# A transformer block with product-key experts: load and router seams reordered, key distances squared by ScalarE in the U tiles with gate groups

## What is computed

```python
def peer(xn, wq, subkeys, u, v):
    def chunk_fn(xc):
        q = (xc @ wq).reshape(PEER_CHUNK, PEER_HEADS, 2, PEER_QDIM // 2)
        sc = jnp.einsum('thpd,pkd->thpk', q, subkeys)
        sv, si = lax.top_k(sc, PEER_TOPK)
        cand = sv[:, :, 0, :, None] + sv[:, :, 1, None, :]
        cv, ci = lax.top_k(cand.reshape(PEER_CHUNK, PEER_HEADS, PEER_TOPK * PEER_TOPK), PEER_TOPK)
        i1 = jnp.take_along_axis(si[:, :, 0], ci // PEER_TOPK, axis=-1)
        i2 = jnp.take_along_axis(si[:, :, 1], ci % PEER_TOPK, axis=-1)
        e = i1 * PEER_NKEYS + i2
        g = jax.nn.softmax(cv.astype(jnp.float32), axis=-1)
        act = jax.nn.gelu(jnp.einsum('td,thkd->thk', xc, u[e]))
        return jnp.einsum('thk,thkd->td', g * act, v[e])
```

## Time and profile before

| what | before |
|---|---|
| median of 3 runs | 1064.41 us |
| the profiled execution | 1065.53 us |
| its span | 1063.7 us |
| busy: TensorE, VectorE, ScalarE, GpSimd | 99%, 82%, 65%, 30% |
| one 128x512 square of ScalarE in the U groups (L1084), and one relu (L1101) | 0.62 us each |
| bytes moved | 181.36 MB, mean 170 GB/s |
| TensorE clock granted | full in all 40 slices |

### The profile page before, as it was taken

One profiled execution on the slowest core, in us unless ns is written; L12 is line 12 of the kernel. 1 busy time (PEld: TensorE's weight loads), 2 busy tenths in 40 slices (PEclk: granted clock), 3 DMA queues, 4 the chain that ended last, 5 costly groups with the idle time before them and its releaser, 6 DMA issues.

```text
span 1063.7 us, 22280 instructions
## 1 busy us (share of the span) xinstructions
PE 1051.3 (99%) x7172; PEld 955.5 (90%) x7172; DVE 874.5 (82%) x1691; ACT 692.0 (65%) x1233; POOL 323.6 (30%) x278
## 2 busy tenths in 40 slices
PE   8999999999999999999999999999999999999998
PEld 6698989999999999999999999888888888888887
DVE  6578786779999988989999999999999995444444
ACT  5366776664444444477777777899999995445553
POOL 0000211007000116633333333134444444554453
PEclk9999999999999999999999999999999999999999
DMA  7753323654455565544444444455444455555553
GB/s 260 269 179 123 117 99 104 196 194 163 146 183 186 178 197 179 181 153 159 158 158 158 158 158 158 148 173 174 158 161 168 165 197 185 192 196 197 187 192 114
DMA packets 50017, 181.36 MB, mean 170 GB/s; under 512 B 5552, under 2 KB 5680, under 8 KB 49968
## 3 DMA queue, kind: packets, MB, share of 16 engines
q1 hardware_dynamic: 49968, 180.74, 50.6%
HBM read 178.62 MB, written 2.10 MB: 170 GB/s over the span
## 4 chain that ended last, share of the span: by engine, by line
PE 94%; DVE 3%; DMA 1%; ACT 1%; issue 0%; POOL 0%; SPq 0%; ACTq 0%; POOLq 0%; DVEq 0%
PE bank L802 33%; PE bank L745 11%; PE bank L747 11%; PE bank L746 11%; PE bank L759 5%; PE bank L350 4%; PE bank L351 3%; PE bank L352 3%; PE bank L683 2%; PE bank L378 1%; PE bank L379 1%; PE bank L380 1%; PE bank L660 1%; PE bank L662 1%; PE bank L661 1%; PE bank L535 1%
## 5 line engine op out<-in xcount | busy, mean ns | idle before, releaser
L1071 ACT ACTIVATE hi<-raw 128x1024 fp32r<-128x1024 f32 x253 | 268.0, 1060 | 244.9 <-PE bank L747 151.1
L1533 DVE TENSOR_TENSOR lo<-raw,hi 128x1024 fp32r<-128x1024 f32 x253 | 314.5, 1247 | 102.8 <-ACT hi L1071 102.0
L745 PE MATMUL bank<-xhi,hi 128*128 128x256 f32 x1024 | 293.9, 287 | 1.3 <-DVE lo L1533 0.7
L747 PE MATMUL bank<-xhi,lo 128*128 128x256 f32 x1024 | 290.4, 284 | 0.0
L746 PE MATMUL bank<-xlo,hi 128*128 128x256 f32 x1024 | 290.1, 283 | 0.0
L1802 POOL TENSOR_TENSOR auxl<-big,auxh 128x256 fp32r<-128x256 f32 x126 | 167.4, 1329 | 200.5 <-ACT auxh L1107 200.5
L745 PEld LDWEIGHTS bank<-xhi,hi 128*128 128x128 f32 x1024 | 196.8, 192 | 2.5 <-issue 1.1
L746 PEld LDWEIGHTS bank<-xlo,hi 128*128 128x128 f32 x1024 | 196.6, 192 | 0.0
L747 PEld LDWEIGHTS bank<-xhi,lo 128*128 128x128 f32 x1024 | 196.3, 192 | 0.0
L802 PE MATMUL bank<-hi,auxh 128*128 128x512 f32 x508 | 160.9, 398 | 0.5 <-POOL auxl L1802 0.3
L802 PE MATMUL bank<-hi,auxl 128*128 128x512 f32 x508 | 157.4, 391 | 0.0
(11 more groups left out here) (307 smaller groups left out, 1697.7 us busy)
## 6 DMA issues: line engine op xcount, KB each, us to landing
raw<-u_d SPq DMA_DIRECT2D x128, 512.0 KB, 3.3
raw<-v_d SPq DMA_DIRECT2D x128, 512.0 KB, 3.2
raw<-wpre_d SPq DMA_DIRECT2D x78, 512.0 KB, 4.2
big<-x_d SPq DMA_DIRECT2D x2, 512.0 KB, 4.6
out_d<-big SPq DMA_DIRECT2D x2, 512.0 KB, 5.2
big<-out_d SPq DMA_DIRECT2D x2, 512.0 KB, 5.0
out_d<-big SPq DMA_DIRECT2D x4, 256.0 KB, 2.1
big<-cst_d SPq DMA_DIRECT2D x1, 735.5 KB, 10.1
```

The costliest lines, as they stand in the source:

```text
L745: pe.matmul(out, wh, xhi[:, k, :], start=(k == 0), stop=False)
L747: m = pe.matmul(out, wl, xhi[:, k, :], start=False, stop=(k == KT - 1))
L1071: act.activation(hi[:, slot(n), :], raw[:, n % RING, :], ACT.Copy).then_inc(hi_done, 1)
L1533: dve.tensor_tensor(lo[:, slot(n), :], raw[:, n % RING, :], hi[:, slot(n), :].bitcast(F32), ALU.subtract).then_inc(lo_done, 1)
```

## The change

1. SP loads both halves of x first, then the constants; eps is set by a VectorE memset and has its own semaphore.
2. The eight `T_W1` tiles leave the ring. They go to `w1`, a free part of `big`, with a semaphore each, and are issued behind the loads of tiles 5, 7, 10, 12 and 14. Ring slots are counted over split tiles alone, and every ring load waits for `lo_done`.
3. `normalise` folds the branch gate into the scaling; GpSimd's first operation of pair 0 also waits for the probabilities of both its heads.
4. Router: one subtraction ahead of the remaining `choose_keys`; the key numbers are transposed before the router's weights; the subtractions of U tiles 63 and 64 come before the first weight rows.
5. In the U tiles with groups ScalarE uses `squares_b`, two groups ahead, around its copy of the next tile; `distances` and `fold_b` are gone, and ScalarE reaches the last two copies of this stage in another order.
6. In the middle of V one `auxh` copy comes before the copy of tile HALF + 2.

```diff
@@ SP
-            sp.dma_start(h[:, 0, :], x_d[0:P, :]).then_inc(x_in[0], 16)
+            for b in range(TB):
+                sp.dma_start(h[:, b, :], x_d[b * P:(b + 1) * P, :]).then_inc(x_in[b], 16)
             sp.dma_start(kep[:, :], kep_d).then_inc(kep_in, 16)
-            sp.dma_start(h[:, 1, :], x_d[P:2 * P, :]).then_inc(x_in[1], 16)
...
+            w1_between = {5: (0, 1), 7: (2, 3), 10: (4, 5), 12: (6,), 14: (7,)}
             for n in range(RING, T_QSB + RING):
-                if is_split(n - RING):
-                    sp.wait_ge(lo_done, splits(n - RING + 1))
-                else:
-                    sp.wait_ge(tile_used, n - RING + 1)
-                load(n % RING, wpre_d[n])
+                if is_split(n):
+                    sp.wait_ge(lo_done, splits(n) - RING + 1)
+                    load(splits(n) % RING, wpre_d[n])
+                for z in w1_between.get(n, ()):
+                    sp.dma_start(w1[:, z, :], wpre_d[T_W1[z]]).then_inc(w1_in[z], 16)
@@ TensorE
-                pe.wait_ge(loaded[n % RING], 16 * (n // RING + 1))
+                pe.wait_ge(w1_in[4 * w + i], 16)
...
+            pe.wait_ge(S("key_numbers"), 32)
+            for w, src in enumerate((i1f, i2f)):
+                for b in range(TB):
+                    m = pe.transpose(bank[6][:, w * T + b * P:w * T + (b + 1) * P], src[:, b * P:(b + 1) * P], ident)
+            m.then_inc(S("keysT"), 1)
             pe.wait_ge(S("router"), 1)
...
+            for b in range(TB):
+                m = pe.transpose(bank[7][:, b * P:(b + 1) * P], gwt[:, b * P:(b + 1) * P], ident)
             m.then_inc(S("routerT"), 1)
@@ ScalarE
-                act.wait_ge(kep_in, 16)
+                act.wait_ge(S("eps"), 1)
...
             def u_step_g(i, j):
-                fold_b(i, j, 1)
+                squares_b(i, j, 2)
                 loop_hi(i, N_PRE + HALF + j + SPLIT)
+                relu_b(i, j, 2)
                 gelu_pair(i, j, HALF)
...
-            fold_b(0, 0, 0)
             for j in range(ROUTER, HALF):
-                u_step(0, j)
-            each_tile(act, HALF - 1, u_step_g)
+                squares_b(0, j - ROUTER, 0)
+                loop_hi(0, N_PRE + j + SPLIT)
+                relu_b(0, j - ROUTER, 0)
+                gelu_pair(0, j, 0)
+            each_tile(act, HALF - 2, u_step_g)
+            loop_hi(0, N_PRE + 2 * HALF - 2 + SPLIT)
...
+            w_hi(0, HALF + 1)
             loop_hi(0, V0 + HALF + 2)
-            w_hi(0, HALF + 1)
@@ VectorE
-                link(dve.tensor_tensor(a_[:, 18:24], a_[:, 18:24], ggate[:, 2 * p + i, :], ALU.mult))
+                g_ = ggate[:, 2 * p + i, :]
...
-                    m = dve.tensor_scalar(x_, x_, a_[:, 18 + c:19 + c], None, ALU.mult)
+                    m = dve.tensor_scalar(x_, x_, a_[:, 18 + c:19 + c], g_[:, c:c + 1], ALU.mult, ALU.mult)
...
+            spread(1)
             for z, c in enumerate(rest):
...
-                spread(TILES_KEYS * (z + 1) // len(rest))
+                spread(1 + (TILES_KEYS - 1) * (z + 1) // len(rest))
@@ GpSimd
                 pool.wait_ge(S("z_read"), p + 1)
+                if p == 0:
+                    pool.wait_ge(S("probs"), 2)
...
-            pool.wait_ge(S("bank67_read"), 2)
-            distances(0, 0, 0)
-            distances(0, 1, 0)
-            each_tile(pool, NGRP - 2, lambda i, j: distances(i, j, 2))
```

63 lines of the change are left out of this document (26 added, 37 removed).

## The result

The changed kernel takes **1058.99 us** (median of 6 runs, 1058.56 to 1061.84), the kernel before, run with it, 1064.60 us (6 runs, 1063.75 to 1065.79). The ratio is 0.9947 with a 95% interval of 0.9936 to 0.9958: 0.5% faster, 5.6 us. Forecast were 1058.9 us and 5.5 us. The profiled execution took 1058.96 us with a span of 1056.8 us, 6.9 us shorter than the span before. (Of the 6.9, about 0.9 is that the execution profiled before, 1065.53 us, lay that far over this median, and 0.4 went to the time around the span: 1.8 us before, 2.2 now. The kernel before has medians of 1064.4 to 1065.6 us in the sets of runs taken beside the experiments, so the 0.9 is no firm figure.)

A forecast was written before the change was run, and what follows sets the result against it. The prediction took TensorE, busy 99% of the span, as the bound. Its terms 0.5 + 1.9 + 0.8 + 0 + 1.2 + 0 + 0.6 + 0.5 = 5.5 us took 1064.41 to 1058.9 us, range 1056.9 to 1061.7.

The forecast's parts named there:

- What bounds the kernel: Whole kernel: TensorE, busy 99% of the span, sets the time; in U tiles with groups VectorE only looks full.
- F: 62 U steps with groups: ScalarE's squares replace GpSimd's distances, TensorE stays at 3.32 us a step; gain 0.
- Rival 4: U steps with groups: VectorE was the bound after all, steps fall to 3.0 us, 19 us more gained, 1040; 4%.
- Rival 3: U steps with groups: ScalarE becomes the bound, steps of 3.62 us, 19 us lost, 1078; 4%.
- B: First-layer compression weights out of the ring: TensorE's two waits for a subtraction go; 1.9 us, range 1.0 to 2.0.
- A: Kernel start: second half of x issued 0.47 us earlier, ahead of the constants; gain 0.5 us, bounds 0 and 0.9.
- C: Softmax seam: folded scaling and GpSimd's wait remove TensorE's wait for the probabilities; gain 0.8 us, lower bound 0.
- rival 1: Softmax seam: GpSimd shut out until all three subtractions are done, C turns from 0.8 gained to 1.3 lost, 1061.0; 10%.
- D: Router start: the 0.7 us wait for a subtraction would turn up again at a later tile; gain 0, at most 0.7.
- E: Router end: earlier key transposes and subtractions, no GpSimd, remove most of 1.34 us of delays; 1.2 us, bounds 0.9 and 1.4.
- G: Start of V: VectorE, freed of GpSimd, weighs the last U group about 0.9 us earlier; gain 0.6, bounds 0.3 and 1.0.
- H: Middle of V: ScalarE makes a weight copy one tile earlier, removing a TensorE gap; gain 0.5 us, bounds 0.3 and 0.6.

The follow-up runs named there:

- best version: Changed kernel plus VectorE's wait for GpSimd's masking at pair 0, its constants wait moved to the identity's scaling, last U group weighed before a subtraction: 1057.51 us.
- three seams undone: Changed kernel with the first loads' order and eps's place, the router-start subtraction's order and the middle-of-V auxh copy's order put back: 1062.38 us.

## Why the prediction was right, and where it was not

The time came out within 0.1 us and the range held. Two parts of that deserve telling apart: the terms that were right, and the errors that cancelled. That they cancelled so closely is luck.

**What bounds the kernel** and **F**: right, and shown. "VectorE only looks full" held exactly: 3.32 us steps with and without GpSimd, the comparison at 415 against 724 ns, a shift that doesn't move over 190 us. The exclusion of VectorE and GpSimd is real and has no price where TensorE is the bound. Rival 4 is out. Rival 3, ScalarE as the bound, had its threshold right (any work over 3.32 us a step lengthens it) and its input wrong: it added four whole durations of 387 ns, while squares follow one another faster than they last. The free time in the trace is 0.32 us a step, about a square and a half.

**B**: 1.9 forecast, 2.01 in the traces, 2.14 by undoing it. The reason, a ring slot held until the tile was used, was the whole of it.

**A**: 0.5 forecast, 0.8 measured (the median of the eleven traces with this order gives 0.8 to 0.9 as well), for a reason I had only half. Not the issue 0.47 us earlier counts but the bytes: with the constants out of the way the second squares start at 5.78 and no longer at 7.54 us, behind ScalarE's own first half. Then TensorE's 32 transposes, 3.5 us long, are the bound. The working said that "only VectorE's scaling by the identity needs" the constants, and took them to be in time. They are not, and VectorE's wait for them stands ahead of two small steps before the scaling as well: the scaling, at 6.47 us in the kernel before, came at 7.14 here and between 6.49 and 8.48 in the other kernels with this order. So the gain of 0.8 us is that of one execution among others from 1.4 us gained to 2.7 lost (last section).

**C**: the one step that failed outright. 0.8 forecast, 0.02 in the table, -0.25 against the seam undone. The working itself put GpSimd's result at 102.9 against a need at 103.1, with "behind VectorE's first subtraction"; it came behind the second, so rival 1 was half right, and deserved more than 10% where the margin was 0.2 us. It was also wrong to count the fold as a pure saving, though most of what C costs, 0.21 of 0.25 us, is GpSimd's wait. Rival 1's price, 1061.0, did not come either: 0.87 us were lost behind the seam where it had 2.1.

**D**: right. The wait at 290.70 is gone, and by 355 us all but 0.1 us is given back.

**E**: 1.2 forecast, 1.48 measured, 0.1 over the upper bound. The order of causes was wrong in part: the forecast gave GpSimd's leaving and the new order together; the runs say that either alone removes the wait behind the first group, that the new order with GpSimd gets a wait of 0.76 us at the group itself, and that only the transposes' 0.43 us needs the order.

**G and H**: 0.6 and 0.5 forecast, 0.38 (0.46 with the step behind) and 0.64 measured. For G the cause, VectorE one group behind, is shown: with GpSimd back 0.61 us are lost there.

**Not seen at all**: 1.42 us in two places. 0.87 of it, in the V steps, comes from the width of `kep`; this is shown (0.86 us with one column more). The diff shows eps leaving `kep`, and I priced it at nothing. The working even took the steady V step of the kernel before as 3.19 us, from a count of groups; start to start it was 3.207. The other 0.55 us, in the attention, is only by elimination put down to eps's place.

**What cancelled**: first, within the sum. C brought 0.8 us less than forecast and G 0.2 less, and A, B, D, E and H brought 0.1 to 0.3 us more each, so that A to H make 5.50 us in the traces against 5.5. Second, outside it. The 1.42 us above stand against the 0.4 us that the time around the span grew by and the 0.9 us by which the execution profiled before was slow. Without the 1.42 us the time would have been about 1060.4 us, 1.5 over the forecast though still in the range.

The listed waits of TensorE add up to 8.9 us before and 4.4 after: more than the 3 us asked for. The watched matmul behind GpSimd was the right one to watch.

## What to carry to other kernels

An engine that shows 100% may be held by a neighbour and not be the bound: look at the spacing of the engine that should wait for it. When two engines exclude each other, give each its turn by a wait rather than hope that one slips in between back-to-back operations: here 1.44 us of waiting saved 0.9. And when a diff moves or resizes a small buffer, all that is laid out behind it moves: pair the same instructions of both traces and look for steps and slopes where no edit is, before crediting a gain to the edit beside it.

## What the hardware showed beyond what was expected

**Turns between VectorE and GpSimd.** GpSimd asked at 97.56 us, ahead of the second subtraction's start at 98.46, and yet that one went first. The Trainium skill, page "SBUF — State Buffer", section "Who interferes with whom", has it that whoever issues first takes the shared ports; by the starts in the trace that does not fit here, where GpSimd's wait is 0.9 us the older, and the measurement decides. In the kernel before, at 461.39 (0.04 us into a subtraction), and in the one with U groups as before, at 459.53 (0.16 us into a subtraction), GpSimd came in behind the first operation, as the lengths of the next ones tell. Consecutive VectorE operations overlap by 0.09 us in all of them. What decides is open.

**A start that depends on when 140 KB land.** With both halves of x ahead of the constants, the identity was scaled between 6.49 and 8.48 us in eleven traces, and the first weight tile began between 11.11 and 15.21; with the old order, in three traces, at 12.52 to 12.62. In two of the eleven TensorE's clock fell as well. The stretch from 7.5 to 12 us in the changed kernel and in the one with U groups as before:

```profile
7.50:12.00 4.50, 4.11 (x34) 3.98 (x35) 2.92 (x8) 2.90 (x8) 0.00 (x0) 1.00 1.02 418
```

```profile
7.50:12.00 4.50, 3.91 (x21) 3.94 (x22) 2.41 (x7) 1.15 (x2) 0.00 (x0) 0.64 1.01 413
```

In the second TensorE had stood still for 1.88 us ahead of the transposes; the granted clock was 0.64 in the mean, and in part of the stretch the transposes started 0.213 us apart in place of 0.111, the lower of the clock's two levels (1.2 and 2.4 GHz). After 0.75 us of standing still, in the changed kernel, it was 1.00, and so it was after 1.84 us in the best version. In the kernel with the weights back in the ring the wait was 3.3 us and the first tile began at 15.21. Five of the 54 runs of these kernels have a mean clock of 0.997 or 0.998 and lie 1.4 to 3.6 us over their kernel's median (1061.84 among the changed kernel's). The two traces are among them: they lie 2.4 and 3.6 us over, and their first tile is 2.0 and 3.5 us later than in the changed kernel. But this isn't shown to come with the new order. With the old one 6 of 62 runs have such a clock too and lie 0.5 to 3.7 us over their median; no trace of one of them was kept. Nor do the other runs scatter more with the new order: five of the changed kernel lie within 0.6 us, ten of a set of the kernel before, at full clock but for one, within 2.8.

**4 bytes.** One column more in `kep`, and a V step takes 3.207 in place of 3.193 us; the same displacement in `big` changes neither this nor GpSimd's 1.55 us. The 1.85 us were seen only in kernels with eps out of `big`, among other differences.

**Time around the span.** A run takes 1.8 us more than its span in the kernel before, in the one with U groups as before and in the one with more work for ScalarE, 1.9 to 2.0 in the one with three seams undone, and 2.1 to 2.2 in the changed kernel and its other variants. No run explains it.
